# Delta-rule chunks: the last stage of a block inversion replaced by forward substitution on the right-hand side, in one kernel of a hybrid encoder step

## The reference, cut to what matters

```python
decay = jnp.exp(jnp.where(incl, gcum[..., :, None] - gcum[..., None, :], -jnp.inf))
kk = jnp.einsum('bhtk,bhsk->bhts', kc, kc)
lhs = eye + jnp.where(strict, bc[..., :, None] * kk * decay, 0.0)
rhs = jnp.concatenate([vc * bc[..., None], kc * (bc * jnp.exp(gcum))[..., None]], axis=-1)
sol = lax.linalg.triangular_solve(lhs, rhs, left_side=True, lower=True, unit_diagonal=True)
u = sol[..., :GDN_DV] - jnp.einsum('bhtk,bhkv->bhtv', sol[..., GDN_DV:], S)
...
o = (jnp.einsum('bhtk,bhkv->bhtv', qc * jnp.exp(gcum)[..., None], S)
     + jnp.einsum('bhts,bhsv->bhtv', attn, u))
k_end = kc * jnp.exp(gcum[..., -1:] - gcum)[..., None]
S = S * jnp.exp(gcum[..., -1])[..., None, None] + jnp.einsum('bhsk,bhsv->bhkv', k_end, u)
```

## Time and profile before

| what | value |
|---|---|
| median of three runs | 2688.94 us (2684.39 to 2692.87) |
| the profiled execution's own time | 2684.61 us |
| its span, first to last instruction | 2682.8 us |
| mean granted TensorE clock | 0.984 |
| TensorE busy | 2507.8 us, 93% |
| VectorE busy | 1007.8 us, 38% |
| ScalarE busy | 707.6 us, 26% |
| a prompt chunk of the delta rule (L1015 of one to L1015 of the next) | 39.17 us |

### The profile page before, as it was taken

The page is one execution under the profiler, slowest core; times in us unless marked ns, Lnnn a source line. Parts: engine busy times, 40 slices in busy tenths (PEclk is TensorE's granted clock), DMA queues, the critical chain, the costliest instruction groups (busy, mean ns, idle before and its releaser), DMA issues.

```text
span 2682.8 us, 39175 instructions
## 1 busy us (share of the span) xinstructions
PE 2507.8 (93%) x16348; PEld 1558.3 (58%) x16348; DVE 1007.8 (38%) x1782; ACT 707.6 (26%) x1251; POOL 64.3 (2%) x66
## 2 busy tenths in 40 slices
PE   6998999999999999999999999999997899989994
PEld 3555888885555566555555556765455444434443
DVE  4356455452223055552332548722245001101115
ACT  3132222221111111120243046731024122222224
POOL 0000000000000000000000000000000000000003
PEclk9999999999999999999999999999997999999998
DMA  7000212204000111141003011131306556657436
GB/s 314 32 32 35 75 44 107 75 31 159 32 32 32 35 52 61 65 156 72 32 18 151 32 38 40 40 116 67 109 23 267 222 208 269 233 231 284 176 129 228
DMA packets 65269, 291.99 MB, mean 109 GB/s; under 512 B 8956, under 2 KB 32068, under 8 KB 44612
## 3 DMA queue, kind: packets, MB, share of 16 engines
q1 hardware_dynamic: 52996, 255.92, 25.2%
q0 software_dynamic: 8928, 22.03, 2.4%
q10 hardware_dynamic: 3168, 11.54, 1.1%
HBM read 694.20 MB, written 56.63 MB: 280 GB/s over the span
## 4 chain that ended last, share of the span: by engine, by line
PE 80%; DMA 7%; DVE 6%; ACT 4%; issue 2%; SPq 1%; POOL 0%; DVEq 0%; ACTq 0%; POOLq 0%
PE psum L531 30%; PE psum L675 16%; PE psum L1519 8%; DMA arena<-in_moe 6%; PE psum L1377 4%; PE psum L1503 4%; PE psum L1102 3%; PE psum L630 2%; ACT arena L1758 1%; PE psum L560 1%; PE psum L1090 1%; PE psum L1015 1%; PE psum L991 1%; PE psum L1488 1%; PE psum L1082 1%
## 5 line engine op out<-in xcount | busy, mean ns | idle before, releaser
L531 PE MATMUL psum<-arena 128*128 128x384 f32 x2544 | 826.6, 487 | 10.9 <-DVEq L330 6.1
L531 PEld LDWEIGHTS psum<-arena 128*128 128x128 f32 x2544 | 483.0, 190 | 352.7 <-issue 10.2
L675 PE MATMUL psum<-arena 128*128 128x384 f32 (+1 forms) x1920 | 537.1, 425 | 6.4 <-ACT arena L689 3.3
L675 PEld LDWEIGHTS psum<-arena 128*128 128x128 f32 x1920 | 339.6, 191 | 152.9 <-ACT arena L689 4.5
L1519 PE MATMUL psum<-arena 128*32 128x256 f32 x5632 | 325.4, 387 | 34.2 <-DMA arena<-in_moe 33.0
L1519 PEld LDWEIGHTS psum<-arena 128*32 128x32 f32 x5632 | 178.8, 112 | 167.0 <-DMA arena<-in_moe 39.0
L1503 PE MATMUL psum<-arena 128*32 128x512 f32 x1408 | 160.5, 594 | 9.9 <-DMA arena<-in_moe 9.2
L1927 ACT ACTIVATE arena<-psum 32x512 f32<-32x512 f32 x174 | 102.2, 588 | 226.9 <-PE psum L1503 225.3
L1377 PE MATMUL psum<-arena 128*128 128x512 f32 (+1 forms) x384 | 126.0, 487 | 0.3 <-issue 0.3
L2623 DVE TENSOR_TENSOR arena<-arena,psum 128x256 f32<-128x256 f32 x44 | 18.5, 421 | 280.7 <-PE psum L1519 190.2
L689 ACT ACTIVATE arena<-psum 128x384 f32<-128x384 f32 x96 | 46.6, 489 | 274.6 <-PE psum L675 214.2
(11 more groups left out here) (541 smaller groups left out, 2402.7 us busy)
## 6 DMA issues: line engine op xcount, KB each, us to landing
arena<-in_moe SPq DMA_DIRECT2D x532, 1024.0 KB
arena<-in_ada SPq DMA_DIRECT2D x12, 2048.0 KB, 9.3
gate_raw<-arena SPq DMA_DIRECT2D x96, 192.0 KB, 1.8
arena<-gate_raw SPq DMA_DIRECT2D x8, 2304.0 KB, 8.4
y_rows<-arena ACTq DMA_DIRECT2D x22, 512.0 KB
arena<-in_gate SPq DMA_DIRECT2D x5, 2048.0 KB, 8.6
arena<-in_br SPq DMA_DIRECT2D x4, 2048.0 KB, 8.1
arena<-in_qkv SPq DMA_DIRECT2D x3, 2048.0 KB, 16.2
```

Of the source, the lines that this page charges most:

```text
L531: last = nc.tensor.matmul(pset(s)[:, n, :], w[:, kk, :], src[:, kk, n * N3:(n + 1) * N3], start=(kk == 0), stop=(kk == K - 1))
L675: last = nc.tensor.matmul(bank(6 + u % 2)[:, cols * p:cols * (p + 1)], w[:, m % 4, kk, :], HT[:, kk, n * N3 + cols * p:n * N3 + cols * (p ...
```

## The change

In the prompt chunks, and there alone, the last of the three stages no longer extends the inverse. After two stages the inverse of the four 32-row diagonal blocks is known. The third stage now makes, with one product per head (L1090's operands exchanged), a matrix that VectorE subtracts from the identity and writes to `cPS` (ScalarE's copy L1631 is gone in that stage). Then three steps run down the right-hand side: step i multiplies 32 columns of `cPS`, all 128 rows deep, with `cVB`, and puts the four heads' 32 by 128 results into the four column groups of one PSUM bank. VectorE copies heads 0 and 1 and ScalarE heads 2 and 3 back into rows 32(i+1) to 32(i+2) of `cVB`. The steps before that, of 128 by 128 with VectorE's subtraction, are gone in this stage. L1122 stays, with the inverse of the diagonal blocks.

The table of filler changes in prompt chunks: 11 in place of 13 at the start, 2 after each of the three solve steps (before 1, 1 and none), none at "w" (before 2). The sum stays 40. The wait for the last `c_x` moves from before `ada_rows` to behind it, with a new wait for ScalarE's part (`c_xt`).

```diff
@@ gdn_fill_points
-        counts = [("start", 13), ("ops", 4)]
+        counts = [("start", 13 if last else 11), ("ops", 4)]
...
-            counts += [("turn%d" % st, 2), ("right%d" % st, 1)] + [("step%d_%d" % (st, i), 1) for i in range(steps - (st == len(STEPS[c])))]
-        counts += [("w", 2), ("o", 2)]
+            counts += [("turn%d" % st, 2), ("right%d" % st, 1)]
+            if st == SOLVE:
+                counts += [("step%d_%d" % (st, i), 2) for i in range(steps)]
+            else:
+                counts += [("step%d_%d" % (st, i), 1) for i in range(steps - (last and st == len(STEPS[c])))]
+        counts += [("w", 2 if last else 0), ("o", 2)]
@@ TensorE
-                        pe.wait_ge(c_xt, 2 * n + 1 + f)
+                        pe.wait_ge(c_xt, 2 * n + 3 * c + 1 + f)
...
-                            last = nc.tensor.matmul(bank(5 * f)[:, hs[e]], cLK[lv % 2][:, hs[h]], gX[h],
-                                                    start=True, stop=True)
+                            left, right = (gX[h], cLK[lv % 2][:, hs[h]]) if lv == SOLVE else (cLK[lv % 2][:, hs[h]], gX[h])
+                            last = nc.tensor.matmul(bank(5 * f)[:, hs[e]], left, right, start=True, stop=True)
...
+                    if lv == SOLVE:
+                        for i in range(steps):
+                            if i:
+                                pe.wait_ge(c_x, 2 * (at + i))
+                                pe.wait_ge(c_xt, 2 * (n + 1) + 3 * c + i)
+                            else:
+                                pe.wait_ge(c_ps, 2 * n + 2)
+                            for h in range(GH):
+                                o = h * P + 32 * (i + 1)
+                                last = nc.tensor.matmul(bank(1 + i % 2)[32 * h:32 * h + 32, 0:P], cPS[:, o:o + 32], cVB[:, hs[h]],
+                                                        start=True, stop=True)
+                            last.then_inc(c_d, 2)
+                            fill(c, "step%d_%d" % (lv, i))
+                        continue
...
-                pe.wait_ge(c_x, 2 * (STEP0[c][-1] + STEPS[c][-1]))
                 if not sample:
                     pe.wait_ge(s_awl, 16 * (c + 1))
                     ada_rows(pe, 0, AWL)
+                    pe.wait_ge(c_xt, 2 * STAGE0[c + 1] + 3 * (c + 1))
+                pe.wait_ge(c_x, 2 * (STEP0[c][-1] + STEPS[c][-1]))
@@ ScalarE
-                    for f in range(2):
-                        act.wait_ge(c_p, 2 * n + 1 + f)
-                        nc.scalar.activation(cPS[:, 256 * f:256 * (f + 1)], bank(5 * f)[:, 0:256], ACT.Copy).then_inc(c_ps, 1)
+                    if lv != SOLVE:
+                        ...
                     evict(c, "right%d" % lv)
                     for i in range(steps):
+                        if lv == SOLVE:
+                            act.wait_ge(c_d, 2 * (STEP0[c][lv - 1] + i + 1))
+                            for h in (2, 3):
+                                last = nc.scalar.activation(cVB[32 * (i + 1):32 * (i + 2), h * P:(h + 1) * P],
+                                                            bank(1 + i % 2)[32 * h:32 * h + 32, 0:P], ACT.Copy)
+                            last.then_inc(c_xt, 1)
@@ VectorE
+                    if lv == SOLVE:
+                        for f in range(2):
+                            dve.wait_ge(c_p, 2 * (STAGE0[c] + lv - 1) + 1 + f)
+                            tt(hd(cPS[:, 256 * f:256 * (f + 1)], 2), by(ident, 2), hd(bank(5 * f)[:, 0:256], 2),
+                               ALU.subtract).then_inc(c_ps, 1)
+                        for i in range(steps):
+                            dve.wait_ge(c_d, 2 * (STEP0[c][lv - 1] + i + 1))
+                            for h in (0, 1):
+                                nc.vector.tensor_copy(cVB[32 * (i + 1):32 * (i + 2), h * P:(h + 1) * P],
+                                                      bank(1 + i % 2)[32 * h:32 * h + 32, 0:P]).then_inc(c_x, 1)
+                        continue
```

More of the change, by code:

```diff
@@ L134 @@
 STEPS = [[3, 3, 3]] * 8 + [[3, 1]]
+SOLVE = 3
 STAGE0 = [sum(len(s) for s in STEPS[:c]) for c in range(NT)]
@@ L1628, in _ @@
                     evict(c, "turn%d" % lv)
-                    for f in range(2):
-                        act.wait_ge(c_p, 2 * n + 1 + f)
-                        nc.scalar.activation(cPS[:, 256 * f:256 * (f + 1)], bank(5 * f)[:, 0:256], ACT.Copy).then_inc(c_ps, 1)
+                    if lv != SOLVE:
+                        for f in range(2):
+                            act.wait_ge(c_p, 2 * n + 1 + f)
+                            nc.scalar.activation(cPS[:, 256 * f:256 * (f + 1)], bank(5 * f)[:, 0:256], ACT.Copy).then_inc(c_ps, 1)
                     evict(c, "right%d" % lv)
                     for i in range(steps):
+                        if lv == SOLVE:
[4 more added lines that the diff above has]
+                            last.then_inc(c_xt, 1)
                         if (c, "step%d_%d" % (lv, i)) in GDN_COUNT:
```

## The result

The changed kernel took 2692.65 us (median of 20 runs, 2683.48 to 2699.78) against 2683.39 us for the kernel before in the same session: ratio 1.0034, 95% interval 1.0024 to 1.0043. It is slower by about 9 us. In the session here and in three later ones, one execution of before lay far off (4412 to 12345 us) and is left out of the ratios. The forecast was 0.9 us faster than before, 2688.0 us against the earlier 2688.94. The time lies in the predicted range, but the direction is wrong. That it lies there is luck: the three runs under the forecast had a median 5.5 us above that of the twenty here, which hides more than half of the loss.

The account below looks back on a forecast made before the run. TensorE was taken to bound the kernel, except at the chunk's start, which is VectorE's. The last stage would take 0.35 + 3 x 1.21 = 3.98 us against 4.09; eight chunks save 0.9, so 2688.94 - 0.9 = 2688.0 us, range 2680 to 2699.

Parts of the forecast that it names:

- What bounds the kernel: Whole span: TensorE busy for 93%; in delta-rule chunks the start is VectorE's, the solve TensorE's, so only less TensorE work helps.
- The subtraction: Last stage, before the first new step: VectorE takes over from ScalarE, and the step starts 0.35 us later.
- The steps: Last stage's three solve steps: 1.21 us of TensorE each, as 0.35 + 0.11 + 0.65 + 0.10.
- the changes of shape: TensorE's switch between full matmuls and four 32-column groups in the last stage: 0.10 us each, 0.54 in the tally.
- the bare loads: First full-matmul load after each step's small products, with nothing to hide behind: 0.11 us per step, 0.33 in all.
- Rival A: Solve steps: the small groups run one after another, step 1.85 us, +14.5 us in all, 2703.4; chance 0.10 in full or part.
- rival B: Solve steps: changes of shape are cheap and steps wait for data, 0.66 us less per chunk, 2683.7; chance 0.10.
- The evictions: Copies out of PSUM after each step: 0.58 us a pair on VectorE, 0.55 on ScalarE, hidden with 0.12 to spare.
- Rival C: Solve steps: slow copy pairs of 0.83 us, +0.26 us a chunk, 2690.1; chance 0.76 together with the forecast.
- The filler: Two matmuls leave the chunk's start, gaining nothing there (idle 0.38 to 1.03 us); the same 0.65 is paid in the steps.
- The sum: Last stage of a prompt chunk: 3.98 us against 4.09, so 0.11 less; 0.9 us over eight chunks.
- Rival D: Prompt chunks: longer TensorE idle at the start lowers the clock, seven chunks lose 26 us, 2714; chance 0.04 with the like.

Follow-up runs that it names:

- before: The kernel without the change, against which ratios are taken: 2683.39 us in the first session; unchanged again 2684.73 us, ratio 1.0004.
- after: The changed kernel, against the kernel without the change: 2692.65 us, ratio 1.0034; run again unchanged 2692.05 us, ratio 1.003.
- five products: Changed kernel with one more 128 by 128 product in five of the eight prompt chunks (1.1 us in all): 2684.18 us, ratio 1.0004.
- ten gave nothing: Changed kernel with ten more 128 by 128 products (2.2 us) in the last prompt chunk: 2695.49 us, ratio 1.0037.
- products at the six waits: 65 unused products ahead of waits outside the delta-rule chunks, added to the changed kernel with 13 filler at the start: 2673.92 us, ratio 0.9969.

## Why the prediction was wrong

- *What bounds the kernel.* Right for the delta-rule part. TensorE is busy for 93% of the whole span too. Outside the chunks the forecast took that busy time as fixed, and it was not.
- *The subtraction.* Forecast: the first step 1.56 us after the first product. Seen: 1.57 (321.30 to 322.87), with TensorE waiting 0.18 for L2169.
- *The steps.* Forecast 1.21 us, seen 1.20. The small groups run at once, and the changes of shape and the bare loads cost what the nearest rows gave. Rival A (1.85) and rival B (1.1) are out.
- *The evictions.* Forecast 0.58 and 0.55 for a pair, seen 0.59 and 0.55; steps two and three wait for nothing. Rival C is out. The bound of which the Trainium skill warns ("TensorEngine Tiling (Array Packing)", "PSUM Bottleneck") did not come: no step waited for a copy.
- *The filler.* Forecast: idle time 1.03 ahead of L1063's successor, seen 1.02 ahead of L1068; `ada_rows` 5.18 after the first product, where 5.2 was forecast. The filler table alone cost 0.6 per chunk in before; back at the start it gained 1.0 in after. The 1.0 is filler and a change of shape saved, together. The sum was 0.11 less per chunk, seen 0.14. In the tally of where the gain goes, the changes of shape should stand at 0.59 (3 x 0.13 and 2 x 0.10), not 0.54; the sum doesn't use that figure.
- *The failed step* is the one that carried the sum to the whole kernel: the forecast is eight times the saving of a chunk and nothing else, with the reason that the rest of the kernel shares no instruction with the change. That term was put at nothing, and 11 us came from it: in the profiled executions 1.2 us ahead of the first chunk, 1.5, 1.6, 1.7 and 3.0 behind four idle waits, and 2.2 behind 2020 us, against 1.0 that seven chunks saved. Rival D, the clock, was looked for only inside the chunks, where it stayed at 1.00, and was given 0.04. The rows that would have warned were in the trace of before: the granted clock was 0.78 in the 7 us behind the idle 2.98 us at 1517, and 1.00 behind the idle 2.87 at 1791. Two nearly equal waits with different outcomes say that the outcome is not fixed by the wait.
- *What is shown and what isn't.* Shown: the lost time of the profiled execution is time at the lower clock, most of it behind unchanged idle waits, and filling such waits keeps the clock up there and takes the loss away. Open: what decides, for a given kernel, which of these waits is followed by a fall. Adding TensorE work doesn't settle it one way (five products gave 8 us, ten gave nothing), and lengthening the execution by a little at its end changed nothing. It differs between kernels even ahead of the first changed instruction: over 20 to 60 us the granted clock was 0.96 in before and 0.91 in after, with the same waits (the two rows below).

```profile
20.00:60.00 40.00, 33.99 (x172) 0.96 0.82 344
```

```profile
20.00:60.00 40.00, 34.05 (x168) 0.91 0.82 345
```

The runs of one kernel differ too: after's fastest, 2683.48 us, had a mean clock of 0.984, its slowest, 2699.78, had 0.977. The Trainium skill, "TensorE: Matmul & The Clock Gate", section "Part 1: The HAM clock gate", says that the gate's rhythm doesn't begin with the kernel and so differs from run to run; the spread of after's runs agrees with it, but the pattern that stays with one kernel (below) is more than that page tells. The trace of before could have warned of a term outside the chunks; it gives neither its size nor its sign.

The best version is the changed kernel with 13 filler matmuls at the chunk's start and products at the six waits: 2673.92 us, ratio 0.9969 to before. Without those products it stands at 0.9978.

## What to carry to other kernels

A change that saves a tenth of a per cent on TensorE can lose three times that in phases it doesn't touch, if they contain idle waits of TensorE of 1 to 3 us: before looking for a new wait, compare the start of the same instruction in both traces, place by place, and the granted clock in windows that begin there. The busy time of unchanged groups is a first hint only, since a record can grow by its modelled end (2.1 of the 4.1 us above). Before judging so small a change, fill such waits with products that nobody reads, in both versions; what is left is the change itself. Filler has a value only where the wait it fills ends last: two matmuls moved from the chunk's start to its last stage cost 0.6 us a chunk.

## What the runs showed of the hardware

- Behind an idle 3.10 us of TensorE near 1141 us the granted clock of the next 7 us was down in all eleven traces in which nothing filled the wait (0.56 to 0.77). Behind the idle 2.98 us near 1518 it was 1.00 in two of eleven, 0.76 to 0.80 in six and 0.56 in three. Behind the idle 2.40 us near 1661, never filled, it was 1.00 in seven of fifteen and 0.76 in eight.
- After an idle 2.87 us of TensorE, at the same matmul near 1791 us, the granted clock of the next 7 us was 1.00 in eight of eleven traces in which nothing filled the wait, and 0.56 or 0.57 in three (after, its repeat, and after with copies at its end). After the idle 0.89 us near 672 it was 1.00 in five of fifteen, 0.76 to 0.79 in nine, and 0.57 in one.
- The pattern stayed with the kernel in its two traces (after: 0.79, 0.56, 0.57; again 0.79, 0.56, 0.56; before: 1.00, 0.78, 1.00; again 1.00, 0.80, 1.00), and five products of 0.22 us changed it.
- With twelve or thirteen products of 128 by 128 right ahead of the wait (2.84 to 3.16 us) the clock was 1.00 in all twelve windows behind them (four traces each near 1141, 1518 and 1791 us). Near 1791 this says little, since eight of eleven empty waits had 1.00 too.
- Two rounds of four products, 32 output rows by 128 columns each, take 0.35 us from the first to the next full matmul (322.87 to 323.22), where eight full records take 0.89. Of the step's 1.20 us, 0.65 is filler and 0.20 is left for the change of shape and the bare load behind it.
